# Block 2 as one block of instructions, the first 128 tokens ahead of the others at every stage

## The reference

```python
for l in range(2):
    xn = rms_norm_2(x, norm1_g[l])
    x = x + mixing_sublayer(xn, ...)[l]     # z = xn @ w_in; three kinds of heads; norm by head; @ w_out
    xn = rms_norm_2(x, norm2_g[l])
    x = x + peer_ffn(xn, ...)[l]
# stick-breaking attention, 6 heads of 64 (before: key index < query index)
z = q @ k.T * scale
log_keep = where(before, -softplus(z), 0)
w = where(before, exp(log_sigmoid(z) + (reversed cumsum(log_keep) - log_keep)), 0);  y = w @ v
# mLSTM, 6 heads: qk = (q @ k.T) * exp(dmat - m_t); y = (qk @ v) / max(|sum(qk)|, exp(-m_t)), causal
# spatial gating, 4 groups: y = u * ((w_s * tril) @ v + b_s) within each 128 tokens
# peer_ffn: for each token and each of 8 heads
q = xn @ wq;  scores against 2 x 128 keys;  top 16 of each side;  top 16 of the 256 sums
y = sum over 16 picks of  gelu(xn . u_tab[i]) * softmax gate * v_tab[i]
```

## Time and profile before

| | |
|---|---|
| median of 3 runs | 2563.07 us (2557.56 to 2566.62) |
| the profiled execution | 2566.87 us, its span 2565.1 us |
| PE, DVE, ACT, POOL busy | 83%, 70%, 32%, 28% |
| mean DMA rate | 274 GB/s |
| mean granted TensorE clock | 0.924 |

### The profile page before, as it was taken

How to read it: one execution, slowest core, us unless ns; L and a number is a source line. 1 busy time by engine, 2 the same in 40 slices (tenths; PEclk the granted TensorE clock), 3 DMA queues, 4 the chain that set the end, 5 groups by cost and what they waited for, 6 DMA issues and landing times. The chain is left out here.

```text
span 2565.1 us, 27636 instructions
## 1 busy us (share of the span) xinstructions
PE 2124.0 (83%) x8423; PEld 1362.4 (53%) x8428; DVE 1801.2 (70%) x4273; ACT 821.5 (32%) x1968; POOL 707.3 (28%) x669
## 2 busy tenths in 40 slices
PE   8689998789978877997877887788779877788777
PEld 7469987469978766532323332277665333333222
DVE  4767774757767544887878777576548878787775
ACT  4456654456655521111111111056211111111110
POOL 0220001210000312354443443113124544434431
PEclk9799999799999769999899999997799999999999
DMA  6144524124526226999999999752269999999996
GB/s 221 66 158 150 194 107 149 39 92 178 189 102 201 85 91 247 379 411 421 421 421 421 421 421 421 321 158 96 91 252 377 409 422 421 421 421 421 421 421 286
DMA packets 138667, 701.79 MB, mean 274 GB/s; under 512 B 14392, under 2 KB 38200, under 8 KB 66616
## 3 DMA queue, kind: packets, MB, share of 16 engines
q0 software_dynamic: 73728, 536.90, 50.7%
q1 hardware_dynamic: 64824, 163.53, 18.0%
HBM read 699.34 MB, written 1.05 MB: 273 GB/s over the span
## 5 line engine op out<-in xcount | busy, mean ns | idle before, releaser
L2097 PE MATMUL bank<-ARENA 128*128 128x512 f32 x2048 | 997.8, 635 | 242.4 <-DVE ARENA L2253 242.1
L2097 PEld LDWEIGHTS bank<-ARENA 128*128 128x128 f32 x2048 | 389.4, 200 | 841.7 <-DVE ARENA L2253 462.9
L2241 DVE CUSTOM_DVE_ANT_0 ARENA<-ARENA 128x1024 f32<-128x1024 f32 x512 | 626.0, 1223 | 225.8 <-DMA ARENA<-in_uv_rows,ARENA 218.8
L2057 POOL DMA_INDIRECT ARENA<-in_uv_rows,ARENA x512 | 544.1, 1063 | 775.9 <-PE bank L2097 676.5
L158 PE MATMUL bank<-PARTS,PARTS 128*128 128x256 f32 (+3 forms) x1488 | 486.7, 327 | 47.3 <-DVE PARTS L1417 17.1
L159 PE MATMUL bank<-PARTS,PARTS 128*128 128x256 f32 (+6 forms) x1600 | 515.9, 324 | 0.0
L160 PE MATMUL bank<-PARTS,PARTS 128*128 128x256 f32 (+6 forms) x1600 | 514.8, 323 | 0.0
L2140 ACT ACTIVATE ARENA<-ARENA 128x1 f32<-128x1 f32 x512 | 103.0, 203 | 1026.1 <-DVE ARENA L2241 1026.1
L158 PEld LDWEIGHTS bank<-PARTS,PARTS 128*128 128x128 f32 x1488 | 286.8, 193 | 74.5 <-DVE PARTS L1417 21.0
L159 PEld LDWEIGHTS bank<-PARTS,PARTS 128*128 128x128 f32 (+2 forms) x1600 | 312.1, 196 | 17.6
L160 PEld LDWEIGHTS bank<-PARTS,PARTS 128*128 128x128 f32 (+2 forms) x1600 | 311.6, 196 | 18.4
(11 more groups left out here) (247 smaller groups left out, 2012.1 us busy)
## 6 DMA issues: line engine op xcount, KB each, us to landing
ARENA<-in_w_up_tiles SPq DMA_DIRECT2D x44, 1024.0 KB, 5.7
ARENA<-in_w_down SPq DMA_DIRECT2D x44, 512.0 KB, 3.6
ARENA<-in_w_in SPq DMA_DIRECT2D x32, 512.0 KB, 7.8
ARENA<-in_w_out SPq DMA_DIRECT2D x32, 512.0 KB, 7.7
ARENA<-in_wq_tiles SPq DMA_DIRECT2D x16, 1024.0 KB, 10.4
ARENA<-in_w_in SPq DMA_DIRECT2D x40, 384.0 KB, 3.8
ARENA<-in_w_in SPq DMA_DIRECT2D x32, 256.0 KB, 3.2
ARENA<-in_uv_rows,ARENA POOLq DMA_INDIRECT x512, 23.0
```

The lines of the kernel that those rows point to most:

```text
L2057: nc.gpsimd.indirect_dma_start(out=slot[i % SLOTS], out_offset=None, in_=table[:, :], in_offset=bass.IndirectOffsetOnAxis(ap=picked[:, t, ...
L2097: last = nc.tensor.matmul(bank[2 * t + n][:, :], diag[i % (2 * QUAD)], slot[i % SLOTS][:, D + n * 512:D + (n + 1) * 512], start=(c == 0), ...
L2241: last = v.tensor_tensor_reduce(u, u, xn[:, t, :], 1.0, 0.0, ALU.mult, ALU.add, dots[:, t, c:c + 1])
```

## The change

Blocks 2 to 5 of each layer become one block, `mixing_out`. Its instruction lists take tile 0 (t = 0) ahead of tile 1 at every stage. Heads are taken in five groups, two of tile 0 with three heads and three of tile 1 with two, so an instruction is 384 or 512 columns wide; scores of an even and an odd group alternate matmul by matmul, 128 columns each. Masks shrink to 128 x 128: the mask is multiplied only into the diagonal blocks, in place, and causal terms go into PSUM by a matmul with the identity. POOL makes half of the output weights' low parts. Slots 4 to 11 lie where the output weights were. Ring of diagonals: 4. In `mixing_in` the values are written straight into `vaug`, the mLSTM values are the last chunk, the output gate's sigmoid is taken inside it, and the output weights are asked for at its end. The next layer's loads wait for row 248.

```diff
+            in_chunks = [..., ("rows", 2304, 384, og), ("rows", 1920, 384, vaug[:, :, :, 0:HD])]
+                        if (c, k) == (9, 6):
+                            act.wait_ge(S("in2_taken_dve"), 9)
+                            nc.scalar.activation(og, og, ACT.Sigmoid)
+            groups = [(0, (0, 2, 4)), (0, (1, 3, 5)), (1, (0, 2)), (1, (1, 3)), (1, (4, 5))]
+            N_DIAG = 4
+            steps = [(0, (0,)), (1, (0,)), (2, (0, 1)), (0, (1,)), (3, (0, 1)), (1, (1,))] + [(h, (0, 1)) for h in range(4, PH)]
+            step_after_row = {1: 2, 9: 3, 17: 4, 25: 5, 33: 6, 49: 7, 65: 8, 81: 9}
...
+                def sp(sp):
+                    load_wq(sp, 0)
...
+                    load_wq(sp, 1)
+                    load_wq(sp, 2)
+                    sp.wait_ge(S("x_xn"), NT)
+                    load_wq(sp, 3)
+                    for h in range(4, PH):
+                        sp.wait_ge(S("q_filled"), step_of[1, h - 4] + 1)
+                        load_wq(sp, h)
+                    if next_loads:
+                        sp.wait_ge(S("row_used"), 248)
+                        next_loads(sp, 0, PIECES)
...
+                    mask(0)                     # POOL
+                    mask(1)
+                    y_root(0)
+                    mask(2)
+                    low(8)
+                    low(9)
+                    mask(3)
+                    for n in range(10, 16):
+                        low(n)
+                    x_root(0)
+                    mask(4)
+                    y_root(1)
+                    for i, (t, c) in enumerate(rows):
+                        if i == 0:
+                            pool.wait_ge(S("sb_values"), N_GROUPS)
+                            pool.wait_ge(S("ml_values"), N_GROUPS)
+                        if i == 4:
+                            x_root(1)
+                            pool.wait_ge(S("out2_done"), 2 * NT)
+                        if i % TOPK == 0:
+                            pool.wait_ge(S("picked_ready"), i // TOPK + 1)
+                        if i >= SLOTS:
+                            pool.wait_ge(S("row_used"), i - SLOTS + 1)
...
+                    def suffix_sums(j):
+                        if t == 0:
+                            last = mm(sb_bank[j][:, 0:n], const("suffix"), lg[j], start=True, stop=True)
+                        else:
+                            mm(..., const("suffix"), first, ...)
+                            mm(..., const("ones"), second, ...)
+                            last = mm(..., const("suffix"), second, ...)
...
+                    sb_scores(0)                # TensorE; sb_scores and ml_scores take two groups
+                    ml_rows(0)
+                    ml_rows(1)
+                    ml_scores(0)
+                    gates()
+                    suffix_sums(0)
+                    suffix_sums(1)
+                    ml_values(0)
+                    ml_values(1)
+                    sb_values(0)
+                    sb_values(1)
+                    sb_scores(2)
+                    ml_rows(2)
+                    ml_rows(3)
+                    turn_y(0)
+                    out(0, 0)
+                    suffix_sums(2)
+                    suffix_sums(3)
+                    ml_scores(2)
+                    out(0, 1)
+                    ml_values(2)
+                    ml_values(3)
+                    sb_values(2)
+                    sb_values(3)
+                    sb_scores(4)
+                    ml_rows(4)
+                    turn_x(0)
+                    ml_scores(4)
+                    queries(0)
+                    suffix_sums(4)
+                    ml_values(4)
+                    sb_values(4)
+                    turn_y(1)
+                    key_scores(0)
+                    out(1, 0)
+                    out(1, 1)
+                    queries(1)
+                    key_scores(1)
+                    turn_x(1)
+                    for i in range(len(rows)):
+                        add_row(i)
+                        if i in step_after_row:
+                            queries(step_after_row[i])
+                        if i - 4 in step_after_row:
+                            key_scores(step_after_row[i - 4])
...
+                    high(0, 2)                  # ScalarE
+                    magnitudes(0, 1)
+                    logs(0, 1)
+                    high(2, 5)
+                    ml_weight(0)
+                    ml_weight(1)
+                    sb_weight(0)
+                    sb_weight(1)
+                    high(5, 8)
+                    y_squares(0)
+                    magnitudes(2, 3)
+                    ml_weight(2)
+                    ml_weight(3)
+                    logs(2, 3)
+                    high(8, 10)
+                    y_high(0)
+                    high(10, 16)
+                    sb_weight(2)
+                    sb_weight(3)
+                    x_squares(0)
+                    magnitudes(4)
+                    ml_weight(4)
+                    logs(4)
+                    take_x(0)
+                    take_queries(0)
+                    sb_weight(4)
+                    y_squares(1)
+                    y_high(1)
+                    take_scores(0)
+                    gate_exp(0)
+                    take_queries(1)
+                    x_squares(1)
...
+                    scaled(0)                   # VectorE
+                    scaled(1)
+                    gated()
+                    low(0, 2)
+                    softplus(0)
+                    softplus(1)
+                    ml_probs(0)
+                    ml_probs(1)
+                    sb_arg(0)
+                    sb_arg(1)
+                    low(2, 5)
+                    scaled(2)
+                    scaled(3)
+                    low(5, 8)
+                    y_sums(0)
+                    softplus(2)
+                    softplus(3)
+                    y_scaled(0)
+                    y_low(0)
+                    sb_arg(2)
+                    sb_arg(3)
+                    ml_probs(2)
+                    ml_probs(3)
+                    add_mixed(0)
+                    scaled(4)
+                    normed(0)
+                    take_x(0)
+                    softplus(4)
+                    ml_probs(4)
+                    sb_arg(4)
+                    y_sums(1)
+                    y_scaled(1)
+                    y_low(1)
+                    first_choice(0)
+                    second_choice(0)
+                    numbers(0)
+                    add_mixed(1)
+                    normed(1)
+                    first_choice(1)
+                    second_choice(1)
+                    take_x(1)
+                    numbers(1)
+                    for i in range(len(rows)):
+                        row_dots(i)
+                        if i >= 1:
+                            diagonal(i - 1)
+                        if i % TOPK == 11 and u < len(units):
+                            first_choice(u)
+                        if i % TOPK == 15 and u < len(units):
+                            second_choice(u)
+                        if i % TOPK == 3 and AHEAD <= u - 1 < len(units):
+                            numbers(u - 1)
```

More of the change, by code:

```diff
@@ L1333, in second_layers, with region @@
-            row_at = take(8 * T)
-            XN_AT = 40960
-            xn = shaped(XN_AT, NT, D)
+            HEADS_AT, WQ_AT, XN_AT, KEYS_AT, GATES_AT, WORK_AT = 16384, 24576, 32768, 34816, 36864, 38688
+            SLOTS_AT = [HEADS_AT + s * 2 * D for s in range(4)] + [(s - 4) * 2 * D for s in range(4, SLOTS)]
+            slot = [arena(at, 2 * D) for at in SLOTS_AT]
+            def region(at, *sizes):
+                starts = [at + sum(sizes[:i]) for i in range(len(sizes))]
+                return starts
@@ L1664, in second_layers @@
             ring = [0] * PIECES
             for l in range(L):
-                w_out = a["w_out_2"][l].rearrange("(k p) n -> p k n", p=P)
                 first = mixing_in(l, ring)
                 ring = [ring[q] + len(range(q, first.pieces, PIECES)) for q in range(PIECES)]
+                after = [ring[q] + 1 for q in range(PIECES)]
+                rest_of = mixing_out(l, ring, mixing_in(l + 1, after).load if l + 1 < L else None)
+                ring = after
                 pre = pre_norm("pre2", None, l, 2, xn, first=0)
@@ L2331, in constants @@
     put("mask_sw", np.where(np.abs(tok[:, :, None] - keys) <= 128, 0.0, -BIG))
-    before = tok[:, :, None] < keys
+    before = p[:, None] < p
     put("strict01", before)
     put("strict_big", np.where(before, 0.0, BIG))
-    put("causal_big", np.where(tok[:, :, None] <= keys, 0.0, BIG))
+    put("causal_big", np.where(p[:, None] <= p, 0.0, BIG))
     put("tril_t", p[:, None] <= p[None, :])
```

1315 lines of the change are left out of this document (589 added, 726 removed).

## The result

The changed kernel takes 2545.7 us (median of 4 runs, 2541.25 to 2547.0) beside 2561.22 for the kernel before (4 runs): a ratio of 0.9935, 95% interval 0.9915 to 0.9954. It is 15.5 us faster, where 45 were forecast; the range (2490 to 2553) held the time, the size was off by two thirds. A second measurement gave 2545.34 beside 2559.99, ratio 0.9942 [0.9925, 0.9958].

What follows compares the result with a forecast made beforehand. DMA transfers were taken to bound each layer's long gather stream, so time saved ahead of the first gather arrives whole at the end. 2566.87 - 53.4 + 7 + 1 = 2521.5 us, as a median 2518; range 2490 to 2553.

Steps and rivals of the forecast that it cites:

- Chain to the first gather: Block start to first gather, tile 0's dependent steps on all engines: 105 us, against 133.7 and 129.7 before.
- bounds of 95 and 120: First gather at 95 if 64-row groups overlap and hops are cheaper; 120 if some 40 hops cost 0.35 more each.
- Start of the stream: First rows behind the first gather: 3 us lost where it was 8.6 before, so -5.6 a layer.
- Query weights in the stream: Five 1024 KB query loads moved behind the first gather: 12.5 us by bytes, taken as 10 a layer.
- The discount: Loads in the stream cost less than by bytes: layer 0's 3.07 MB, 7.3 us by bytes, added only 4.4.
- The -1.5 for the next loads: Layer 0's stream: the next layer's loads leave four rows later and share less, -1.5 us.
- Next layer's loads: Weights may land 1 us late at the next layer's first casts; the moved sigmoid hides: +1 in all.
- Ring of four: Four diagonals for eight in the stream: costs nothing while 12 slots cover 30 us, otherwise up to 2 a step.
- The 53.4 of the forecast: Gain ahead of the first gather over both layers, 28.7 + 24.7 us; 73.4 and 23.4 at the bounds.
- Early rows starve: Rival: query steps and choices crowd rows 0 to 34, losing 20 us a layer instead of 3; 2552, chance 0.10.
- The gain is eaten: Rival: hops 0.35 dearer each (120), weights at full price with 8 lost; 2563, no change, chance 0.07.
- Half clock throughout: Rival: TensorE stays at half clock through the block, first gather at 146; 2621, chance 0.05.

Runs made afterwards that it cites:

- x_sem: Changed kernel with the drain between the two POOL instructions of `x_root` replaced by a semaphore wait; 2528.0 us, ratio 0.9872 to the kernel before.
- no_loads: Changed kernel without the four query-weight loads (heads 4 to 7) inside each stream, so queries are wrong; 2518.2 us, ratio 0.9842 to the kernel before.
- zeros_back: Changed kernel with one more product, result unused, for each of tile 0's two groups in the suffix sums; 2544.2 us in one run.
- tile1_first: Changed kernel with the second token tile's last steps put back ahead of the first choice; 2559.0 us, ratio 0.9992 to the kernel before.

## Why the prediction was wrong

The direction, the mechanism and layer 0's first gather were right; the sum missed 19.8 us against its own profiled run. By its steps:

- **Chain to the first gather, 105 in both layers.** Layer 0 was 104.7. Layer 1's 111.1 is the late place of the clock: 6 us, inside the bounds of 95 and 120. The mean of the 16 layers is 107.6. The single prices were not as good as the sum. The first 18 score matmuls run from 859.13 to 860.28, 0.064 us each at full clock, where I took 0.11. The Trainium skill (TensorEngine Tiling (Array Packing), Key Properties) says that different tiles load weights and multiply in parallel; the estimate that I worked out by it and set aside, 6 us for 108, is 0.055 each, and this trace is nearer to it than to 0.11. It saved little, since TensorE then stood 4.2 us for the masks.
- **Start of the stream, -5.6 a layer: the step that failed.** I counted POOL's queue as four gathers, then `x_root(1)`, and gave the root its two instructions. I said what stands behind the wait, but put no price on the drain, which behind indirect DMAs is a wait until they have landed. The fifth gather came at 15.4 in place of 10, over the 15 that I had named as the sign of being wrong. With the drain replaced (x_sem) the stream is 7.0 and 6.2 shorter, and the rest of the step stands: the early loss falls from 11.3 to 3.7, -7.6 where I said -5.6 (my 8.6 of before counted only 80 of the first 160 us). The drain is 13.2 us over two layers.
- **Query weights in the stream, +10 and +8.5: mis-sized.** By no_loads, which saved 20.2 over two layers with four loads in each, five loads cost 12.6 a layer, near the price by bytes (5.24 MB, 12.4); for head 3's that is carried over, not measured. The discount came from one comparison: layer 0's stream, with 3.07 MB of the next layer's weights, was only 4.4 longer than layer 1's. Up to the dot of row 240 the two are equal (621.9 and 622.0 us). The difference arises in the end, shown here by the last 40 us ahead of the last dot in the trace of the kernel before:

```profile
1619.72:1659.72 40.00, 29.38 (x58) 10.02 (x57) 21.31 (x44) 2.84 (x14) 4.78 (x5) 0.96 0.85 338
2512.54:2552.54 40.00, 30.76 (x63) 10.69 (x63) 23.80 (x51) 3.24 (x16) 6.75 (x7) 1.00 0.75 310
```

  Neither is at 421: the last gathers leave room, and 28 GB/s for 40 us, 1.1 MB of the 3.07, went into it. The other 2 MB at 421 are 4.6 us, beside the 4.4 measured, so there was no discount in a full stream. The -1.5 for the next loads did not come either: 3.03 MB of them still lie in layer 0's stream. In all 6.7 us.
- **Next layer's loads, +1:** 102.93 beside 102.98, nothing (the further traces have 104.3 and 105.5 before, 105.4 after). Ring of four: nothing, right. Removed products: no price given, 2.6 and 2.7 by zeros_back.
- **The balance.** The streams missed 17.7 (24.7 for 7), of which the two causes explain 19.9; the 2.2 over are the better rest of the start. With 5.9 at the first gathers, less 2.3 for layer 0's earlier start, 1 for the loads and 0.5 behind the last dots, that is the 19.8.
- **The base.** I laid the gain on one trace of the kernel before, and carried it to the median by a constant. That execution took longer than all four timed runs of its kernel. Over six layers in three traces its first gather is at 129.6 in the mean; the changed kernel's is at 108.3 over four: 21.3 a layer. The streams' means are 662.1 and 675.0, 12.9 more. Twice the difference is 17 us, beside 15.5 and 14.7 measured; this is where the missing 10 lie. The 53.4 of the forecast could not have been had against the median.
- **Rivals.** "Early rows starve" (2552) was nearest in time and in place, by another mechanism: it was to come from crowded query steps behind row 1, and came ahead of row 0. "The gain is eaten" had the weights at full price, rightly. Half clock throughout did not come, but half clock in the stretch from 20 to 50 us is the late place.

## What to carry to other kernels

When small work is put between DMA issues in one queue, price the drains in it as the time until all that the queue has issued has landed (9.4 to 22.6 us here), and use a semaphore of the instruction itself where one value is all that is waited for. Where the DMA is the bound, each byte moved into the stretch costs its full share; a discount needs its own evidence. Forecast from more than one trace if the clock switches in the stretch: here the first gather of the kernel before lay at three places, 12 us from the first to the last. Compare traces of two kernels only where the granted clock of the stretch is the same: tile1_first looked 13.4 us later by the mean and was 16 by like layers.

## What the runs showed of the hardware, unexpected

- A drain in POOL's queue stood 9.4 us behind four indirect DMAs in flight, 1.0 behind one that was nearly in, 16.2 behind eight and up to 22.6 in the full stream; a semaphore wait in its place 0.08. The small instruction behind the drain started 0.30 to 0.31 us behind the landing of the last gather, in 14 of 14 layers.
- The same code got a granted clock of 0.84 or 0.50 in the same 10 us, in different layers and runs, and the first gather moved by 5 to 6 us with it; 16 layers of one chain fall on three places (104.7 to 104.9, 106.1 to 106.3, 110.9 to 111.2).
- Interleaved 64-row matmuls of an even and an odd head at 128 columns: 0.064 us each, where split-float ones of 128 rows and 160 columns took 0.11.
